# RWKV chunk tail and scan: a dense dummy matmul in every job and every step, and the scan's preparation spread anew

## The chip, the cores and the metric

The program runs on one core of one Trainium2 chip. The metric is device time in microseconds (us) of one execution; lower is better.

## The reference: what is computed

One layer of a diffusion backbone on 1152 tokens (1024 of a sample, 128 of a prompt): a SwiGLU half step, a mixer, another SwiGLU half step, with norms between. The mixer adds a Fourier group and a bidirectional RWKV-7 group with 8 heads of 64 channels. The change lies in the RWKV group, whose core is this scan, run forward and in reverse for every head:

```python
def step(state, inp):
    r_t, w_t, k_t, v_t, kk_t, a_t = inp
    sa = jnp.einsum('bhvk,bhk->bhv', state, -kk_t)
    state = (state * w_t[:, :, None, :]
             + sa[..., None] * (kk_t * a_t)[:, :, None, :]
             + v_t[..., None] * k_t[:, :, None, :])
    return state, jnp.einsum('bhvk,bhk->bhv', state, r_t)
```

kk is k scaled and divided by its norm in each head; w and a come from small products (64 wide) through a sigmoid.

## The kernel before

The heads are taken two at a time, as four pairs p = 0 to 3, one after the other. The 1152 tokens are 18 chunks of 64 (NCH = 18). Each pair goes through three stages, and a stage begins only when every engine has ended the one before:

- **rw_chunks** makes what each chunk needs by itself. TensorE (PE) works through a list of jobs written out by hand, each a handful of small matmuls into one of eight PSUM banks (12 f32 matmuls in an f, w or y job, 6 in a u job), and ScalarE (ACT) or VectorE (DVE) copies each bank out. Meanwhile DVE inverts small triangular matrices, first for direction 0, then for direction 1. The list ends with two tails, one for each direction: 3 f jobs, 3 w jobs, 6 u jobs and 3 y jobs. The f jobs of a direction need DVE's inverse (`nat0_1`, `nat1_1`), and four dummy matmuls of 512 columns stand before that wait (`keep_clock(pe, sb, out, 4)`).
- **rw_scan** runs the 18 chunks in order, both directions (d) in turn. In step i PE makes S (old state times the chunk's keys, L1753), DVE adds to it (L1797), PE makes M from it (L1762), and DVE makes the new state (L1804) with GpSimd's decayed old one (L1817). Y is two more groups on PE (L1767, L1771), and ACT copies it out (L1826). S of a step needs M of the step before from DVE, and ACT's copy of Y, for its PSUM bank. PE's order is S0, S1, M0, Y0, M1, Y1.
- **rw_turn** finishes the pair and turns the prepared data of the next one into scan operands.

For p = 0 to 2 the scan also prepares the next pair, in class **Prep**: at the end of each step PE, ACT and DVE do the pieces that a table gives them. PE has 16 pieces, one in each of steps 1 to 16: `ss` (sums of squares, 9 matmuls with 128x128 weights and 2 columns, L1149, after ACT's `sq`), six `a`, six `w` (one matmul of 384 columns, L1228), and three `kk` (3 matmuls of 128 columns, L1157). DVE has passes over 128x1152 (`kd`, `ak`, `kds`, `rkk`: L1285, L1288, L1297, L1300) and two scans (`scan0`, `scan1`, L1292). **rw_first** runs the same pieces alone for the first pair.

An f32 matmul is two instructions in the trace, each with a weight load (PEld).

Of the kernel before, what the change touches and what calls it, by code (L numbers as in the profile page):

```python
# [8 lines left out]
ALU = mybir.AluOpType  # L9
# [5 lines left out]
P = 128  # L15
# [5 lines left out]
NT = T // P  # L21
# [106 lines left out]
    return pe.matmul(out, w_hi, x_hi, start=False, stop=stop)  # L128


def keep_clock(pe, sb, out, n):

    for _ in range(n):
        pe.matmul(out, sb["cst"][:, C_ID:C_ID + P], sb["cst"][:, 0:512], start=True, stop=True)


def parts(c):
# [1005 lines left out]
    return t[:, ::-1] if d else t  # L1143


def head_sums(pe, sb, ps, x):

    for t in range(NT):
        last = pe.matmul(ps[:, 2 * t:2 * t + 2], x[:, t * P:(t + 1) * P], sb["cst"][:, C_BLK:C_BLK + P:HS],  # L1149
                         start=True, stop=True)  # L1150
    return last
# [15 lines left out]
PP = {n: i for i, n in enumerate(("w0_0", "w0_1", "a0_0", "a0_1", "k_k", "k_a", "r_k", "ln_w", "ln_b", "one_ka"))}  # L1167


class Prep:  # L1170

    ITEMS = ["ss"] + [f"{n}_{c}" for n in ("a0", "kk", "w0", "a1", "w1") for c in range(NC)]

    def __init__(self, st, io, sb, rw, zd, p, ps):

# [5 lines left out]

    def items(self, i):

        return self.ITEMS[i - 1:i] if i else []

    def act_names(self, i):
        out = [x for x in self.items(i) if x[0] in "wa"]
        return out + {2: ["sqrt"], 5: ["kda0"], 14: ["kda1"]}.get(i, [])  # L1190

    def dve_names(self, i):
        out = [x for x in self.items(i) if x[0] not in "wa"]
        return out + {3: ["inv", "wide"], 6: ["kd0"], 9: ["ak0"], 12: ["scan0"], 15: ["kd1"], 16: ["ak1"],
                      17: ["kds", "rkk", "scan1"]}.get(i, [])

    def of(self, name):
        return (self.act_t if name[0] in "wa" else self.dve_t)
# [12 lines left out]
    def pe(self, pe, i):  # L1211
        rw = self.rw
        for name in self.items(i):
            n = self.ITEMS.index(name)
            if n >= 2:
                before = self.ITEMS[n - 2]
                self.of(before).wait(pe, before)
            bank = self.ps[:, n % 2, :]
            if name == "ss":
                self.act_t.wait(pe, "sq")  # L1220
                last = head_sums(pe, self.sb, bank, rw.sq[:, :])
            else:
                c = int(name[-1])
                if name[0] in "wa":
                    d, which = int(name[1]), "wa".index(name[0])
                    rows = slice(HS * d, HS * d + HS)
                    pe.wait_ge(self.w_in[which], 16)
                    last = pe.matmul(bank[:, 0:CW], (rw.w2, rw.a2)[which][rows, :], rw.lora[rows, which, c * CW:(c + 1) * CW],  # L1228
                                     start=True, stop=True)
                else:  # L1230
                    self.dve_t.wait(pe, "wide")
                    last = spread(pe, self.sb, bank, rw.sq[:, :], c)
            self.pe_t.did(name, last)

    def act(self, act, i):
        rw, t = self.rw, self.act_t
        if i == 0:
            act.wait_ge(self.z_in[1], 16)
            self.dve_t.wait(act, "ka1")
            t.did("kraw", act.activation(rw.kk[:, :], rw.rkv[:, 1, :], ACT.Identity, scale=self.par("k_k")))  # L1240
            t.wait(act, "kraw")
            t.did("sq", act.activation(rw.sq[:, :], rw.kk[:, :], ACT.Square))
        for name in self.act_names(i):
            if name == "sqrt":
                self.dve_t.wait(act, "ss")
                t.did(name, act.activation(rw.inv[:, :], rw.inv[:, :], ACT.Sqrt))
            elif name.startswith("kda"):
                d = int(name[-1])
                t.wait(act, f"a{d}_{NC - 1}")
                t.did(name, act.activation(rw.bk[:, d, :, 1, :], by_chunk(rw.ai[d]), ACT.Identity, bias=self.par("one_ka"),  # L1250
                                           scale=self.par("k_a")))
            else:
                d, c = int(name[1]), int(name[-1])
                self.pe_t.wait(act, name)
                dst = (rw.sw if name[0] == "w" else rw.ai)[d]
                t.did(name, act.activation(dst[:, c * CW:(c + 1) * CW], self.ps[:, self.ITEMS.index(name) % 2, 0:CW],
                                           ACT.Sigmoid, bias=self.par(f"{name[0]}0_{d}")))

    def dve(self, dve, i):
# [7 lines left out]
            t.did("ka1", dve.tensor_scalar(self.par("one_ka"), self.par("k_a"), -1.0, 1.0, ALU.mult, ALU.add))  # L1267
        for name in self.dve_names(i):
            d = int(name[-1]) if name[-1].isdigit() else None
            if name == "ss":  # L1270
                self.pe_t.wait(dve, "ss")
                ins = dve.tensor_scalar(rw.inv[:, :], self.ps[:, 0, 0:2 * NT], 1e-24, None, ALU.max)
            elif name == "inv":
                self.act_t.wait(dve, "sqrt")
                ins = dve.reciprocal(rw.inv[:, :], rw.inv[:, :])
# [3 lines left out]
            elif name.startswith("kk_"):  # L1279
                self.pe_t.wait(dve, name)  # L1280
                cols = slice(d * CW, (d + 1) * CW)
                ins = dve.tensor_tensor(rw.kk[:, cols], self.ps[:, self.ITEMS.index(name) % 2, 0:CW], rw.kk[:, cols], ALU.mult)
            elif name.startswith("kd") and d is not None:
                self.act_t.wait(dve, f"kda{d}")
                ins = dve.tensor_tensor(rw.bk[:, d, :, 1, :], rw.bk[:, d, :, 1, :], by_chunk(rw.rkv[:, 1, :]), ALU.mult)  # L1285
            elif name.startswith("ak"):
                t.wait(dve, f"kk_{NC - 1}")
                ins = dve.tensor_tensor(rw.bk[:, d, :, 0, :], by_chunk(rw.ai[d]), by_chunk(rw.kk[:, :]), ALU.mult)  # L1288
            elif name.startswith("scan"):
                t.wait(dve, f"ak{d}")  # L1290
# [182 lines left out]
def rw_chunks(nc, io, sb, rw, nd, wd):  # L1473
# [44 lines left out]
    with Stage(nc) as st, nc.psum_tensor(fresh("g_ps"), [P, 8, 512], F32) as ps:  # L1518
# [10 lines left out]
        with st.block() as block:  # L1529
# [37 lines left out]
            def _(pe):  # L1567
                for n, (k, d, q) in enumerate(jobs):
# [31 lines left out]
                                             start=True, stop=True)  # L1600
                    elif k == "f":
                        if q == 0:
                            keep_clock(pe, sb, out, 4)
                            dve_t.wait(pe, f"nat{d}_1")
                        for j in range(NF):
                            u = q * NF + j
                            last = pe.matmul(out[second(d), j * B:(j + 1) * B], gu[first(d), d, u, second(d)],
                                             nat[d][first(d), u, :], start=True, stop=True)
                    elif k == "w":
                        copied(pe, "f", d, q)  # L1610
                        for j in range(NF):
                            u = q * NF + j
                            last = pe.matmul(out[first(d), j * B:(j + 1) * B], fs[d][second(d), u * B:(u + 1) * B],
                                             wu[second(d), d, u, second(d)], start=True, stop=True)
                    elif k == "u":
                        copied(pe, "z", d, q)
                        copied(pe, "w", d, q * NU // NF)
                        for j in range(NU):
                            u = q * NU + j
                            last = pe.matmul(out[0:HS, j * HS:(j + 1) * HS], wu[:, d, u, :], su[0:HS, d, u, :],  # L1620
                                             start=True, stop=True)
                    else:
                        copied(pe, "a", d, NG - 1)
                        for m in (1, 2):
                            copied(pe, "w", d, m)
                        for j in range(NU):
                            c = q * NU + j
                            for h in range(2):
                                last = pe.matmul(out[HS * h:HS * h + HS, j * HS:(j + 1) * HS],
                                                 at[:, d, c, HS * h:HS * h + HS], rw.wt[:, d, h, c, :], start=True, stop=True)  # L1630
                    pe_t.did(name(k, d, q), last)

            def copy_out(eng, tr, k, d, q, copy, neg):

# [90 lines left out]
def rw_scan(nc, io, sb, rw, zd, p, more):  # L1725
# [4 lines left out]
    SD = [(i, d) for i in range(NCH) for d in range(2)]  # L1730
    y = [rw.work[:, d * T:(d + 1) * T] for d in range(2)]
    with Stage(nc) as st, nc.psum_tensor(fresh("c_ps"), [P, 8, 512], F32) as ps:
        pe_t = Steps(st.sem("pe_s"), [x for i in range(NCH) for x in (f"S{i}_0", f"S{i}_1", f"M{i}_0", f"Y{i}_0", f"M{i}_1", f"Y{i}_1")] +
                     ["st0", "st1"])
        dve_t = Steps(st.sem("dve_s"), ["zero"] + [x for i in range(NCH) for x in
                                                   [f"S{i}_0", f"S{i}_1"] + [f"M{i}_0", f"M{i}_1"]])
# [5 lines left out]
        with st.block() as block:  # L1742
            @block.tensor
            def _(pe):
# [9 lines left out]
                                         old(i, d)[rows], start=True, stop=True)  # L1754
                    pe_t.did(f"S{i}_{d}", last)

                def rest(i, d):
                    c = order[d][i]
                    dve_t.wait(pe, f"S{i}_{d}")
                    for h in range(2):  # L1760
                        rows = slice(HS * h, HS * h + HS)
                        last = pe.matmul(ps[rows, 4 + d, 0:HS], rw.bt[:, d, c, HS * h:HS * h + HS],  # L1762
                                         rw.sv[:, d, h, c, :], start=True, stop=True)
                    pe_t.did(f"M{i}_{d}", last)
                    for h in range(2):
                        rows = slice(HS * h, HS * h + HS)
                        pe.matmul(ps[rows, 2 * d + h, HS:2 * HS], rw.sv[:, d, h, c, :], rw.gr[:, d, h, c, HS:2 * HS],  # L1767
# [3 lines left out]
                        last = pe.matmul(ps[rows, 2 * d + h, HS:2 * HS], old(i, d)[rows],  # L1771
                                         rw.ar[rows, d, 1, c * HS:(c + 1) * HS], start=False, stop=True)
                    pe_t.did(f"Y{i}_{d}", last)
                for i, d in SD:
                    s_part(i, d)
                    if d:
                        rest(i, 0)
                        rest(i, 1)
                        if more:
                            prep.pe(pe, i)  # L1780
                for d in range(2):

                    act_t.wait(pe, f"Y{NCH - 1}_{d}")
# [194 lines left out]
```

## Time and profile before

| | us |
|---|---|
| runs: median (lowest to highest) | 3276.66 (3276.38 to 3277.37) |
| the profiled execution | 3270.4 |
| its span, first to last instruction | 3268.6 |
| PE busy in the span | 2870.4 (88%) |
| DVE / ACT / GpSimd busy | 1469.9 / 782.3 / 105.2 |
| mean granted TensorE clock | 0.857 of full |

The four pairs lie between 1399.4 and about 2250 us of the span. PEclk in the page and in the answers is the clock that was granted to TensorE, as a share of full speed: 1.00 is 2.4 GHz and 0.50 is 1.2 GHz. The instruction rows give the start and the stretch of a merged group, then engine, line, operation, tiles, shapes and count; in brackets stands the idle time before it and what ended it.

### The profile page before, as it was taken

To read this page: it belongs to the slowest core of one execution; us is meant where nothing else is said; L and a number is where in the kernel's file an instruction comes from. 1 tells how busy PE (TensorE), PEld (TensorE's weight loads), DVE (VectorE), ACT (ScalarE), POOL (GpSimd) and SP (SyncE) were. 2 spreads that over 40 slices of the span, in tenths; PEclk is the share of its full clock that TensorE was granted. 3 is DMA by queue.
4 is the path that set the end of the run, shared out by engine and by line. 5 is a ranking of instruction groups with operands and counts; after the bars stand their busy time and mean duration, and the time that the engine had idled before them with its cause. 6 is when DMAs were issued, how large, how long until landed. Compare 5 with 4: busy or idle time off the path is not lost. (4 is left out here: it accounts for less than half of the span.)

```text
span 3268.6 us, 47367 instructions
## 1 busy us (share of the span) xinstructions
PE 2870.4 (88%) x18974; PEld 2642.3 (81%) x18974; DVE 1469.9 (45%) x2799; ACT 782.3 (24%) x1527; POOL 105.2 (3%) x165
## 2 busy tenths in 40 slices
PE   4599999999996999579689688786889999999995
PEld 2289999999995998266476575666789999999995
DVE  1453333333437661382563745733364433333335
ACT  1231111111104111333243433322141111111112
POOL 0000000000000000001102001010000000000000
PEclk7799999999997999765665655657889999999997
DMA  8511111111101232111010110104111111111101
GB/s 350 208 52 39 39 39 39 51 39 50 40 7 40 82 96 106 76 24 31 18 23 24 25 39 3 34 5 162 39 49 42 45 39 39 39 39 51 39 19 58
DMA packets 190799, 182.69 MB, mean 56 GB/s; under 512 B 43956, under 2 KB 163551, under 8 KB 190687
## 3 DMA queue, kind: packets, MB, share of 16 engines
q1 hardware_dynamic: 190416, 180.97, 17.1%
q8 instruction: 87, 1.43, 0.2%
q14 instruction: 26, 0.21, 0.0%
q10 hardware_dynamic: 270, 0.09, 0.0%
HBM read 153.05 MB, written 27.98 MB: 55 GB/s over the span
## 5 line engine op out<-in xcount | busy, mean ns | idle before, releaser
L126 PE MATMUL ff_ps<-h_hi,ff_wlo 128*128 128x384 f32 x2112 | 710.7, 336 | 5.6 <-ACT ff_s L602 5.6
L127 PE MATMUL ff_ps<-h_lo,ff_whi 128*128 128x384 f32 x2112 | 709.9, 336 | 0.0
L128 PE MATMUL ff_ps<-h_hi,ff_whi 128*128 128x384 f32 x2112 | 709.6, 336 | 0.0
L650 DVE TENSOR_TENSOR ff_s<-ff_ps,ff_s 128x384 f32<-128x384 f32 x132 | 73.5, 557 | 750.0 <-PE ff_ps L128 748.7
L126 PEld LDWEIGHTS ff_ps<-h_hi,ff_wlo 128*128 128x128 f32 x2112 | 400.2, 189 | 6.2 <-ACT ff_s L602 6.2
L127 PEld LDWEIGHTS ff_ps<-h_lo,ff_whi 128*128 128x128 f32 x2112 | 399.8, 189 | 0.0
L128 PEld LDWEIGHTS ff_ps<-h_hi,ff_whi 128*128 128x128 f32 x2112 | 399.7, 189 | 0.0
L128 PE MATMUL ff_ps<-ff_uhi,ff_whi 128*128 128x384 f32 x1056 | 352.7, 334 | 0.0
L127 PE MATMUL ff_ps<-ff_ulo,ff_whi 128*128 128x384 f32 x1056 | 352.7, 334 | 0.0
L126 PE MATMUL ff_ps<-ff_uhi,ff_wlo 128*128 128x384 f32 x1056 | 352.7, 334 | 0.0
L602 ACT ACTIVATE ff_s<-ff_ps 128x384 f32<-128x384 f32 x132 | 65.1, 493 | 738.4 <-PE ff_ps L128 738.4
L661 DVE SCALAR_TENSOR_TENSOR x_again<-ff_ps,mod,x_again 128x256 f32<-128x256 f32 (+1 forms) x352 | 171.1, 514 | 72.1 <-PE ff_ps L128 71.4
L661 DVE SCALAR_TENSOR_TENSOR x<-ff_ps,mod,x 128x256 f32<-128x256 f32 (+1 forms) x352 | 171.0, 514 | 72.1 <-PE ff_ps L128 71.4
L606 ACT ACTIVATE ff_uhi<-ff_s 128x384 fp32r<-128x384 f32 x132 | 69.4, 526 | 556.1 <-DVE ff_s L650 556.1
L127 PEld LDWEIGHTS ff_ps<-ff_ulo,ff_whi 128*128 128x128 f32 x1056 | 198.2, 188 | 0.0
L128 PEld LDWEIGHTS ff_ps<-ff_uhi,ff_whi 128*128 128x128 f32 x1056 | 198.2, 188 | 0.0
L126 PEld LDWEIGHTS ff_ps<-ff_uhi,ff_wlo 128*128 128x128 f32 x1056 | 198.2, 188 | 0.0
L643 DVE TENSOR_TENSOR ff_wlo<-ff_raw,ff_whi 128x1024 fp32r<-128x1024 f32 x132 | 157.5, 1219 | 17.7 <-ACT ff_whi L597 17.5
L126 PE MATMUL pj_ps<-h_hi,pj_wlo 128*128 128x384 f32 x456 | 154.2, 338 | 1.5 <-DVE h_lo L464 1.5
L127 PE MATMUL pj_ps<-h_lo,pj_whi 128*128 128x384 f32 x456 | 153.2, 336 | 0.0
L128 PE MATMUL pj_ps<-h_hi,pj_whi 128*128 128x384 f32 x456 | 153.1, 336 | 0.0
L597 ACT ACTIVATE ff_whi<-ff_raw 128x1024 fp32r<-128x1024 f32 x132 | 131.8, 1044 | 0.0
(269 smaller groups left out, 3759.4 us busy)
## 6 DMA issues: line engine op xcount, KB each, us to landing
md_w<-w_mod SPq DMA_DIRECT2D x9, 4096.0 KB, 24.6
ff_raw<-ffn_w_gate SPq DMA_DIRECT2D x44, 512.0 KB, 4.6
ff_raw<-ffn_w_up SPq DMA_DIRECT2D x44, 512.0 KB, 3.9
ff_raw<-ffn_w_down SPq DMA_DIRECT2D x44, 512.0 KB, 3.7
pj_raw<-w_in SPq DMA_DIRECT2D x19, 512.0 KB, 4.0
z_dram<-pj_zo SPq DMA_DIRECT2D x15, 576.0 KB, 2.9
rw_rkv<-z_dram SPq DMA_DIRECT2D x12, 576.0 KB, 5.6
x_dram<-x SPq DMA_DIRECT2D x1, 4608.0 KB, 21.7
```

The costliest lines, as they stand in the source:

```text
L126: pe.matmul(out, w_lo, x_hi, start=start, stop=False)
L127: pe.matmul(out, w_hi, x_lo, start=False, stop=False)
L128: return pe.matmul(out, w_hi, x_hi, start=False, stop=stop)
L597: act.activation(w_hi[:, u, :], raw[:, u % RAW, :], ACT.Copy).then_inc(w_hi_s, 1)
L602: act.activation(silu[:, t % 2, :], ps[:, t % 2, 0:CW], ACT.Silu).then_inc(gate_free, 1)
L606: act.activation(hid_hi[:, m, c * CW:(c + 1) * CW], hid[:, t % 2, :], ACT.Copy).then_inc(hid_hi_s, 1)
L643: dve.tensor_tensor(w_lo[:, u, :], raw[:, u % RAW, :], w_hi[:, u, :].bitcast(F32), ALU.subtract)\
L650: dve.tensor_tensor(hid[:, t % 2, :], ps[:, 2 + t % 2, 0:CW], silu[:, t % 2, :], ALU.mult)\
L661: last = dve.scalar_tensor_tensor(xs, ps[:, 4 + n % 4, a:b], sb["mod"][:, (3 * (2 * f) + 2) * KD + o, s:s + 1], xs, ALU.mult, ALU.add)
```

## The change

1. `keep_clock` takes a number of columns. A dummy multiplies the 128x128 identity with `columns` columns of the constants, into a bank that is written anew afterwards.
2. In rw_chunks every f, w, u and y job of both directions (15 in each) begins with a dummy of 128 columns. The f jobs keep the four of 512 as well. After the last job PE waits for the copy of the eighth-last job and makes two dummies of 512 columns.
3. In rw_scan every step of all four pairs gets a dummy of 256 columns behind S0 and S1, and PE's order becomes S0, S1, dummy, M0, M1, Y0, Y1.
4. Prep's pieces are laid out in three tables. `ss` is cut into three pieces of 3 matmuls, in steps 1 to 3, each together with an `a0` piece; `kk` goes to steps 7 to 9, `w` to 10 to 15. On DVE `kd1`, `kds`, `rkk`, `scan0` and `scan1` move to steps 8, 13, 14, 15 and 16 (they were in 15, 17, 17, 12 and 17). On ACT `sqrt` moves from step 2 to 4, `kda1` from 14 to 7.

```diff
-def keep_clock(pe, sb, out, n):
+def keep_clock(pe, sb, out, columns, n=1):
     for _ in range(n):
-        pe.matmul(out, sb["cst"][:, C_ID:C_ID + P], sb["cst"][:, 0:512], start=True, stop=True)
+        pe.matmul(out[:, 0:columns], sb["cst"][:, C_ID:C_ID + P], sb["cst"][:, 0:columns], start=True, stop=True)
...
+PREP_PE = {1: ("ss_0", "a0_0"), 2: ("ss_1", "a0_1"), 3: ("ss_2", "a0_2"), 4: ("a1_0", ), 5: ("a1_1", ), 6: ("a1_2", ),
+           7: ("kk_0", ), 8: ("kk_1", ), 9: ("kk_2", ), 10: ("w0_0", ), 11: ("w0_1", ), 12: ("w0_2", ),
+           13: ("w1_0", ), 14: ("w1_1", ), 15: ("w1_2", )}
+PREP_ACT = {4: ("sqrt", ), 5: ("kda0", ), 7: ("kda1", )}
+PREP_DVE = {1: ("ss_0", ), 2: ("ss_1", ), 3: ("ss_2", ), 5: ("inv", "wide"), 6: ("kd0", ), 8: ("kk_0", "kd1"), 9: ("kk_1", ),
+            10: ("kk_2", ), 11: ("ak0", ), 12: ("ak1", ), 13: ("kds", ), 14: ("rkk", ), 15: ("scan0", ), 16: ("scan1", )}
...
-    ITEMS = ["ss"] + [f"{n}_{c}" for n in ("a0", "kk", "w0", "a1", "w1") for c in range(NC)]
+    ITEMS = [name for i in sorted(PREP_PE) for name in PREP_PE[i]]
...
                         if q == 0:
-                            keep_clock(pe, sb, out, 4)
+                            keep_clock(pe, sb, out, 512, 4)
                             dve_t.wait(pe, f"nat{d}_1")
+                        keep_clock(pe, sb, out, P)
...
                     elif k == "w":
+                        keep_clock(pe, sb, out, P)
                         copied(pe, "f", d, q)
...
                     elif k == "u":
+                        keep_clock(pe, sb, out, P)
                         copied(pe, "z", d, q)
...
                     else:
+                        keep_clock(pe, sb, out, P)
                         copied(pe, "a", d, NG - 1)
...
                     pe_t.did(name(k, d, q), last)
+                copied(pe, *jobs[-8])
+                keep_clock(pe, sb, ps[:, len(jobs) % 8, :], 512, 2)
...
-                for i, d in SD:
-                    s_part(i, d)
-                    if d:
-                        rest(i, 0)
-                        rest(i, 1)
-                        if more:
-                            prep.pe(pe, i)
+                for i in range(NCH):
+                    for d in range(2):
+                        s_part(i, d)
+                    keep_clock(pe, sb, ps[:, 4, P:3 * P], 2 * P)
+                    for part in (m_part, y_part):
+                        for d in range(2):
+                            part(i, d)
+                    if more:
+                        prep.pe(pe, i)
```

## Rows read from the trace of the kernel before

**Rows 1.** The page, part 2: the span in 40 slices.

```profile
PEclk7799999999997999765665655657889999999997
```

**Rows 2.** Busy time by stage; columns PE, PEld, DVE, ACT, POOL, PEclk, DMA share, GB/s.

```profile
1399.40:1496.90 97.50, 82.72 (x978) 72.78 (x978) 64.10 (x160) 32.69 (x86) 5.89 (x4) 0.69 0.12 26
1496.90:1585.80 88.90, 78.08 (x644) 52.34 (x644) 34.66 (x89) 32.46 (x96) 21.74 (x36) 0.50 0.07 23
...
2148.80:2209.90 61.10, 50.37 (x584) 38.77 (x584) 20.42 (x73) 16.53 (x76) 15.89 (x36) 0.50 0.01 3
```

**Rows 3.** Timeline of PE in pair 0, both tails of the chunk stage.

```profile
1454.22 3.88 PE L1607 MATMUL g_ps<-rw_rkv,rw_gr 32*32 32x32 f32 x69 [5.44 <-DVE rw_rkv L1706]
...
1461.85 7.83 PE L1620 MATMUL g_ps<-rw_sv,rw_wt 64*64 64x64 f32 x71
...
1469.53 4.09 PE L1629 MATMUL g_ps<-rw_wt,rw_bk 64*64 64x64 f32 x71
1473.56 6.17 PE L134 MATMUL g_ps<-cst 128*128 128x512 f32 x8
1479.66 2.37 PE L1607 MATMUL g_ps<-rw_sq,rw_gr 32*32 32x32 f32 x69
...
1484.23 6.89 PE L1620 MATMUL g_ps<-rw_sv,rw_wt 64*64 64x64 f32 x71
...
1490.97 4.09 PE L1629 MATMUL g_ps<-rw_wt,rw_bk 64*64 64x64 f32 x71
```

**Rows 4.** Busy time and granted clock in short stretches, columns as in rows 2.

```profile
1441.00:1444.40 3.40, 3.40 (x62) 3.40 (x60) 2.88 (x13) 3.00 (x8) 0.00 (x0) 1.00 0.00 0
1454.20:1473.50 19.30, 19.28 (x288) 19.15 (x288) 14.20 (x40) 6.76 (x14) 0.00 (x0) 0.50 0.06 18
1473.50:1478.60 5.10, 5.10 (x8) 2.19 (x7) 2.01 (x2) 0.49 (x1) 0.00 (x0) 0.50 0.36 58
1478.60:1482.00 3.40, 3.40 (x80) 2.53 (x79) 1.27 (x2) 0.48 (x1) 0.00 (x0) 1.00 0.00 0
1482.00:1485.40 3.40, 3.40 (x96) 3.36 (x92) 0.55 (x1) 1.67 (x4) 0.00 (x0) 1.00 0.02 5
```

**Rows 5.** Timeline of PE in pair 0's scan, a step with a `kk` piece.

```profile
1523.04 0.48 PE L1762 MATMUL c_ps<-rw_sv,rw_bt 128*64 128x64 f32 x4
1523.30 0.43 PE L1767 MATMUL c_ps<-rw_gr,rw_sv 128*64 128x64 f32 x4
1523.66 0.48 PE L1771 MATMUL c_ps<-rw_ar,rw_m 64*64 64x64 f32 x4
1524.07 1.65 PE L1157 MATMUL c_ps<-cst,rw_sq 128*128 128x128 f32 x6
1525.64 0.69 PE L1753 MATMUL c_ps<-rw_m,rw_ar 64*64 64x64 f32 x8
1526.56 0.48 PE L1762 MATMUL c_ps<-rw_sv,rw_bt 128*64 128x64 f32 x4 [0.22 <-DVE rw_sv L1797]
```

**Rows 6.** Timeline in pair 3's scan, which has no preparation.

```profile
2152.60 0.48 PE L1753 MATMUL c_ps<-rw_m,rw_ar 64*64 64x64 f32 x4 [0.43 <-DVE rw_sv L1797]
...
2154.67 0.37 PE L1771 MATMUL c_ps<-rw_ar,rw_m 64*64 64x64 f32 x2
...
2155.20 0.45 ACT L1826 ACTIVATE rw_work<-c_ps 64x64 f32<-64x64 f32 x2 [0.59 <-PE c_ps L1771]
...
2155.79 0.48 PE L1753 MATMUL c_ps<-rw_m,rw_ar 64*64 64x64 f32 x4 [0.43 <-DVE rw_sv L1797]
```

**Rows 7.** Timeline of pair 0's scan: its start, and the wait for `sq`.

```profile
1497.12 0.70 PE L1753 MATMUL c_ps<-rw_m,rw_ar 64*64 64x64 f32 x8 [2.06 <-DVE rw_m L1792]
...
1503.68 4.00 PE L1149 MATMUL c_ps<-cst,rw_sq 128*128 128x2 f32 x18 [0.37 <-ACT rw_sq L1242]
```

**Rows 8.** Timeline at the end of pair 0's scan.

```profile
1581.31 0.38 SPq L1846 DMA_DIRECT2D state_b<-rw_mp  x1
1582.00 2.55 DVE L1292 TENSOR_TENSOR_SCAN rw_wt<-rw_reset,rw_wt 128x1152 f32<-128x1152 bf16 x1
```

More of the change, by code:

```diff
@@ L1143, in reverse, with head_sums @@
     return t[:, ::-1] if d else t
-def head_sums(pe, sb, ps, x):
-    for t in range(NT):
+def head_sums(pe, sb, ps, x, tiles=range(NT)):
+    for t in tiles:
         last = pe.matmul(ps[:, 2 * t:2 * t + 2], x[:, t * P:(t + 1) * P], sb["cst"][:, C_BLK:C_BLK + P:HS],
@@ L1184, in items @@
     def items(self, i):
-        return self.ITEMS[i - 1:i] if i else []
+        return list(PREP_PE.get(i, ()))
     def act_names(self, i):
         out = [x for x in self.items(i) if x[0] in "wa"]
-        return out + {2: ["sqrt"], 5: ["kda0"], 14: ["kda1"]}.get(i, [])
+        return out + list(PREP_ACT.get(i, ()))
     def dve_names(self, i):
-        out = [x for x in self.items(i) if x[0] not in "wa"]
-        return out + {3: ["inv", "wide"], 6: ["kd0"], 9: ["ak0"], 12: ["scan0"], 15: ["kd1"], 16: ["ak1"],
-                      17: ["kds", "rkk", "scan1"]}.get(i, [])
+        return list(PREP_DVE.get(i, ()))
     def of(self, name):
@@ L1218, in pe @@
             bank = self.ps[:, n % 2, :]
-            if name == "ss":
+            if name.startswith("ss"):
                 self.act_t.wait(pe, "sq")
-                last = head_sums(pe, self.sb, bank, rw.sq[:, :])
+                j = int(name[-1])
+                last = head_sums(pe, self.sb, bank, rw.sq[:, :], range(j * NC, (j + 1) * NC))
             else:
@@ L1244, in act @@
             if name == "sqrt":
-                self.dve_t.wait(act, "ss")
+                self.dve_t.wait(act, "ss_2")
                 t.did(name, act.activation(rw.inv[:, :], rw.inv[:, :], ACT.Sqrt))
@@ L1269, in dve @@
             d = int(name[-1]) if name[-1].isdigit() else None
-            if name == "ss":
-                self.pe_t.wait(dve, "ss")
-                ins = dve.tensor_scalar(rw.inv[:, :], self.ps[:, 0, 0:2 * NT], 1e-24, None, ALU.max)
+            if name.startswith("ss"):
+                self.pe_t.wait(dve, name)
+                cols = slice(d * 2 * NC, (d + 1) * 2 * NC)
+                ins = dve.tensor_scalar(rw.inv[:, cols], self.ps[:, self.ITEMS.index(name) % 2, cols], 1e-24, None, ALU.max)
             elif name == "inv":
@@ L1287, in dve @@
                 t.wait(dve, f"kk_{NC - 1}")
+                self.act_t.wait(dve, f"a{d}_{NC - 1}")
                 ins = dve.tensor_tensor(rw.bk[:, d, :, 0, :], by_chunk(rw.ai[d]), by_chunk(rw.kk[:, :]), ALU.mult)
@@ L1732, in rw_scan @@
     with Stage(nc) as st, nc.psum_tensor(fresh("c_ps"), [P, 8, 512], F32) as ps:
-        pe_t = Steps(st.sem("pe_s"), [x for i in range(NCH) for x in (f"S{i}_0", f"S{i}_1", f"M{i}_0", f"Y{i}_0", f"M{i}_1", f"Y{i}_1")] +
+        pe_t = Steps(st.sem("pe_s"), [x for i in range(NCH) for x in (f"S{i}_0", f"S{i}_1", f"M{i}_0", f"M{i}_1", f"Y{i}_0", f"Y{i}_1")] +
                      ["st0", "st1"])
@@ L1755, in s_part, with m_part @@
                     pe_t.did(f"S{i}_{d}", last)
-                def rest(i, d):
+                def m_part(i, d):
                     c = order[d][i]
@@ L1764, in rest, with y_part @@
                     pe_t.did(f"M{i}_{d}", last)
+                def y_part(i, d):
+                    c = order[d][i]
                     for h in range(2):
```

## Prediction, written before the changed kernel ran

> **What bounds the kernel now.** I read the page's slices first. The clock granted to TensorE is near full at both ends and drops to a half for long parts of slices 18 to 27, where the four pairs lie [rows 1]. A table by stage says where: in the chunk stage the mean grant is 0.69, in both kinds of scan it is 0.50, though PE is busy for 78 of 89 us and 50 of 61 us [rows 2]. So these stages are set by small matmuls at 1.2 GHz and by the hand-overs between engines. The change buys a faster clock with extra PE work. Two questions decide: what a dummy costs, and whether the clock comes.
>
> **The price of a dummy.** It stands in no row, so I build it. In the first tail 72 instructions of 64 columns take 1461.85 to 1469.53, 0.107 us each at the slow clock [rows 3]; 128 columns are then 0.21 us, and a dummy of 128 columns (two instructions) streams for 0.43 us. But a group with 128x128 weights among small ones costs more than its stream. The six instructions of a `kk` piece stream for 1.28 us, and the next group starts 1.57 us after their first: 0.29 us more. Ahead of it, the four instructions of L1771 hold PE for 0.41 us, where the four of L1762 take 0.26 us: another 0.15 us [rows 5]. I take 0.43 + 0.44, about 0.88 us at the slow clock and 0.44 at the fast. The bound below is the stream alone, 0.43 and 0.21 us, if the loads hide; the bound above is 0.95, since a 32x32 group may be slower to restart.
>
> These rows speak against a load that hides. The Trainium skill (TensorE: Matmul & The Clock Gate, Part 2, step 1) says that a weight load is pulled ahead of running matmuls only when its row groups don't conflict or it goes to a background buffer. If it went there, a dummy would cost its stream, and the kernel would land at the second rival below.
>
> **First tail of the chunk stage (direction 0).** PE has no gap in it: 19.3 us busy of 19.3, clock 0.50 [rows 4]. Nothing hides the dummies: 15 x 0.88 = 13.2 us. The wide dummies and the f jobs of direction 1 stand behind it, and DVE's inverse was ready when they came (6.1 us later) [rows 3]. I take 13.0 us, since a wide dummy may see the fast clock a little sooner.
>
> **Second tail.** It begins at the fast clock, which the four wide dummies brought (5.1 us dense at 0.50, then 1.00) [rows 4]. But in before the clock held only to 1485.4, though PE never paused: f1 and w1 are 32x32 [rows 3, 4]. With a dummy in each job, a job is 4.57 / 6 = 0.76 us of small work and 0.44 us of dummy, of which only 0.21 streams. That is a sixth of the time dense, the rest at 32x32, and I take it as too thin: nearest to it is the stretch that lost the clock. A stretch of only 64x64 work (the z jobs) kept it [rows 4], so u and y jobs would hold it, if it lived so long. So: four f and w jobs fast, 4 x 1.2 = 4.8 us; two slow, at 7.63 / 6 + 0.88 = 2.15 each, 4.3; six u at 1.28 + 0.88, 13.0; three y at 1.35 + 0.88, 6.7. Sum 28.8 us, against 15.4 (1479.66 to 1495.06): +13.4. The two dummies of 512 columns at the end are 4 x 0.85 + 0.3 = 3.7 us, less the copy of the last job that they run beside, under 1 us: +2.8.
>
> A pair's chunk stage: 13.0 + 13.4 + 2.8 = +29.2 us; four pairs: **+117**.
>
> **Scan of pairs 0 to 2.** A step of 4.55 us is M, Y, Y twice (0.26 + 0.36 + 0.41, twice), the piece 1.57, and S to M 0.92 [rows 5]. PE is nearly the whole of it. New, slow clock: S 0.38, then 0.24 to the dummy, then 256 columns twice at 0.43 with 0.29 around them, 1.77 in all from S to M instead of 0.92. DVE's add no longer shows, which is the little that the dummy covers. M0 and M1 together save 0.05. So +0.8 a step, 18 steps: +14.4. The cut `ss` adds two changes of weights, +0.5. The later passes of DVE fit beside steps of 5.3 us, so a stall of about a pass (1.3 us) goes, and the stage no longer ends on `kds`, `rkk`, `scan1` (to 1584.55) but on the store of the states issued at 1581.31 [rows 8]: -1.2. Sum +12.4, three pairs **+37**.
>
> Could it run fast? The stage starts with a hole: PE's `ss_0` waits for ACT's `sq` until 1503.68, 6.6 us after the start [rows 7], and at the fast clock two steps are done by 5 us. The hole, and then matmuls of two columns, lose the clock if it was there. In the slow clock the `kk` steps come nearest to winning it back: 1.28 us dense, S, then 0.85 us dense. 1.28 alone never did in before; 5.1 did [rows 4, 5]. I give each scan even odds. A fast step is half of 5.35, about 2.7 us, since PE is nearly all of it. From step 8 on, eight such steps are worth 20 us. The likeliest count is one or two of three: **-28**.
>
> **Scan of pair 3.** A step is 3.19 us (2152.60 to 2155.79), and what ends the wait is ACT's copy of Y1: from the start of Y1's last group to the next S1 it is 1.12 us [rows 6]. The dummy comes behind S1, so it lies on this chain. New period: 1.12, then S1 to dummy 0.40, dummy 1.14, M 0.48, Y0 and Y1 up to that last group 0.36 + 0.77: 4.27 us. 18 x 1.08 = **+19.5**. I take the slow clock: the end of the chunk stage leaves a gap of over 1.5 us before the scan's first S.
>
> rw_first runs the same pieces in the new order, with the same work: within 2 us of none.
>
> **Sum.** 117 + 37 - 28 + 19.5 = +146 us. On the profiled execution's 3270.4 that is 3416; the median of the runs is 6.3 above it, so 3423. I say **3423 us**. Less than 0.2% (7 us) is what a measurement here can't tell from no change.
>
> **Rivals.**
> *The clock holds (faster).* It decides in one place: whether f and w jobs with their dummies keep 1.00 in the second tail, and then the dummies before and in the scan carry it on. Then the second tail is 6 x 1.2 + 6 x 1.08 + 3 x 1.12 = 17.1 us, +1.7; the end +1.0; with 13.0 a pair pays 15.7, four 63. The scans of pairs 0 to 2 run 16 steps at 2.7 instead of 4.55 us, -30, and lose 2 to DVE's longer passes, -28 each; pair 3's chain at 2.7 us (its 3.15 us of PE work halve, of the 1.12 about 1.0 stays, since most of it is ACT), -9. Sum 63 - 84 - 9 = -30: 3247 us. For it: the z jobs' stretch. Against: 1482.0 to 1485.4, PE busy throughout, and the fall behind it [rows 4]. The Trainium skill (the same page, the part on why this matters) asks only that TensorE be kept busy without long gaps; by that rule the second tail would have stayed fast in before too, and the trace differs. Chance 0.12.
>
> *The loads hide.* A dummy costs its stream: first tail +6.4; second 22.2 us, +6.8; end +2.5, four pairs 63. Scans +5 each, pair 3 +12. Sum +90: 3367 us. Against: rows 5 name both extras. Chance 0.07.
>
> *The tail is slow, the scans fast.* The wide dummies at the stage's end bring the clock and it is held: 117 - 93 = +24, 3301 us. The hole at `sq` [rows 7] stands against it for three pairs. Chance 0.07.
>
> *Nothing moves,* gains and costs cancel: 0.02.
>
> **How the numbers follow.** My case has 0.72. Its own range: no scan won back is 3451, all three 3391; a dummy at 0.95 adds 15; 3380 to 3470. The range for 8 in 10 goes down to take in the loads that hide and part of what lies between: 3325 to 3470. Faster 0.12, same 0.02, slower 0.86.
>
> **What would show it.** In the profile after: 0.9 us between the small groups around each dummy in the first tail, and f1 some 13 us later after f0; the grant falling before w1 ends; PEclk 0.50 at step 2 of pairs 0 to 2; steps of 5.3 us, and of 4.3 in pair 3. I'm wrong if the second tail shows 1.00 to its end, if scan steps of 2.7 us fill a stage, or if a dummy costs 0.5 us.

## The result, and the profile after

| | before | after |
|---|---|---|
| median of the runs (us) | 3276.52 (3275.04 to 3277.37) | 3372.74 (3370.30 to 3378.87) |
| ratio, 95% interval | | 1.0297 (1.0279 to 1.0315) |
| the profiled execution / its span | 3270.4 / 3268.6 | 3378.9 / 3377.1 |

The changed kernel is 96 us slower (a prediction of 3423, range 3325 to 3470, against 3372.74). The profiled execution of after is 108.5 us longer than that of before; it lies 6.1 us above its median where before's lay 6.1 below.

The page's slices of after. Between slices 18 and 27 the grant (the clock granted to TensorE) is only a little higher than in [rows 1], digits that average 6.2 against 5.5; the four pairs last longer.

```profile
PEclk7699999999998998567756756767979999999997
...
L134 PE MATMUL g_ps<-cst 128*128 128x128 f32 (+1 forms) x320 | 140.0, 553 | 21.2 <-DVE rw_rkv L1721 21.2
```

The table by stage of after, chunk stage and scan in turn for pairs 0 to 3 (columns as in [rows 2]). A chunk stage runs here from GpSimd's clearing of its tiles to DVE's clearing of `rw_m`, the scan from there to DVE's first addition in rw_turn.

```profile
1402.05:1528.07 126.02, 112.04 (x1042) 92.60 (x1042) 64.12 (x161) 32.72 (x86) 5.89 (x4) 0.64 0.09 20
1528.07:1612.32 84.25, 76.94 (x680) 49.25 (x680) 33.26 (x91) 32.61 (x97) 26.70 (x36) 0.71 0.07 25
1640.98:1771.76 130.78, 113.17 (x1042) 92.09 (x1042) 64.09 (x160) 32.72 (x86) 5.89 (x4) 0.63 0.09 19
1771.76:1857.84 86.08, 80.39 (x680) 51.81 (x680) 33.35 (x92) 32.62 (x97) 26.66 (x36) 0.68 0.07 24
1886.48:2017.46 130.98, 113.24 (x1042) 92.14 (x1042) 64.09 (x160) 32.72 (x86) 5.89 (x4) 0.63 0.09 19
2017.46:2103.53 86.07, 80.40 (x680) 51.79 (x680) 33.35 (x91) 32.63 (x97) 26.66 (x36) 0.68 0.07 24
2131.99:2258.45 126.46, 112.40 (x1042) 92.74 (x1042) 64.17 (x161) 32.72 (x86) 5.89 (x4) 0.64 0.10 20
2258.45:2313.99 55.54, 46.86 (x620) 31.95 (x620) 18.81 (x73) 16.55 (x76) 15.38 (x36) 1.00 0.01 3
```

By the same marks the stages of before last 97.5, 100.6, 101.0, 98.4 us (chunk) and 89.0, 88.7, 88.5, 61.4 us (scan). So:

| stages of four pairs, us | before | after | measured | predicted |
|---|---|---|---|---|
| rw_chunks | 397.5 | 514.3 | +116.8 | +117 |
| scans of pairs 0 to 2 | 266.2 | 256.4 | -9.8 | +37 - 28 = +9 |
| scan of pair 3 | 61.4 | 55.5 | -5.8 | +19.5 |

That is +101.2 us. The other 7.3 of the 108.5 lie outside these stages: 2.6 before the first chunk stage, 0.1 in the three rw_turn between pairs, 4.6 behind the last scan. The change touches none of that code but rw_first, which has the new order of pieces. The profiled executions with the new order reach the first chunk stage between 1398.9 and 1402.1 us, and that of e2 below, with the old one, at 1401.5, so the order doesn't explain the 2.6 us. I take the 7.3 us for a property of these two executions; the medians are 96 us apart.

PE's timeline in pair 0's tails (f1 and w1 are the f and w jobs of direction 1): a slow f job of the first tail, then the start of the second tail, then the end of the list.

```profile
1459.10 0.80 PE L134 MATMUL g_ps<-cst 128*128 128x128 f32 x2
1459.83 1.49 PE L1617 MATMUL g_ps<-rw_rkv,rw_gr 32*32 32x32 f32 x24
1461.24 0.80 PE L134 MATMUL g_ps<-cst 128*128 128x128 f32 x2
...
1489.56 5.03 PE L134 MATMUL g_ps<-cst 128*128 128x512 f32 x10
1494.53 0.94 PE L1617 MATMUL g_ps<-rw_sq,rw_gr 32*32 32x32 f32 x24
1495.40 0.49 PE L134 MATMUL g_ps<-cst 128*128 128x128 f32 x2
...
1498.39 1.31 PE L1624 MATMUL g_ps<-rw_wt,rw_rkv 32*32 32x32 f32 x24
1499.64 0.80 PE L134 MATMUL g_ps<-cst 128*128 128x128 f32 x2
...
1523.68 3.10 PE L134 MATMUL g_ps<-cst 128*128 128x512 f32 x4
1528.29 0.45 PE L1768 MATMUL c_ps<-rw_m,rw_ar 64*64 64x64 f32 x8 [1.51 <-DVE rw_m L1812]
```

A slow job takes 1461.24 - 1459.10 = 2.14 us, where [rows 3] gave 7.63 / 6 = 1.27: the dummy costs 0.87 us. The first tail is 32.6 us (1456.96 to 1489.56) against 19.3. The wide dummies take 5.0 us instead of 6.1, the second tail 29.2 us (1494.53 to 1523.68) against 15.4, and from there to the scan's start it is 4.4 us against 1.8: +13.3, -1.1, +13.8 and +2.6, in all +28.5 us. By the marks above the four chunk stages grow by 28.5, 30.2, 30.0 and 28.0 us.

Busy time and granted clock in pair 0: the second tail's start and its rest, the scan's start, its middle, its end.

```profile
1491.80:1498.60 6.80, 6.80 (x92) 4.73 (x91) 0.55 (x1) 0.96 (x2) 0.00 (x0) 1.00 0.01 2
1498.70:1526.00 27.30, 27.30 (x237) 22.43 (x235) 2.75 (x5) 3.39 (x7) 0.00 (x0) 0.50 0.00 1
1526.00:1536.20 10.20, 6.50 (x77) 4.16 (x75) 2.40 (x11) 4.05 (x10) 2.62 (x6) 1.00 0.54 190
1536.20:1580.60 44.40, 44.40 (x293) 28.03 (x294) 11.96 (x38) 16.34 (x41) 7.69 (x14) 0.50 0.00 1
1580.60:1607.90 27.30, 26.08 (x316) 16.71 (x312) 18.91 (x42) 10.99 (x41) 16.40 (x16) 1.00 0.00 1
```

The grant falls in w1's first job, is back for the end dummies and the scan's first steps, falls at the wait for `sq`, and comes back at 1580.60, behind the second `kk` piece and the dummy of the step after it. These are the rows where it falls and rises (ACT, PE), and the dummies of two steps after it:

```profile
1534.20 1.16 ACT L1249 ACTIVATE rw_sq<-rw_kk 128x1152 f32<-128x1152 f32 x1
...
1535.42 0.83 PE L1149 MATMUL c_ps<-cst,rw_sq 128*128 128x2 f32 x6 [1.88 <-ACT rw_sq L1249]
...
1573.60 1.22 PE L134 MATMUL c_ps<-cst 128*128 128x256 f32 x2
...
1576.82 1.65 PE L1157 MATMUL c_ps<-cst,rw_sq 128*128 128x128 f32 x6
...
1579.02 1.22 PE L134 MATMUL c_ps<-cst 128*128 128x256 f32 x2
...
1581.63 0.94 PE L1157 MATMUL c_ps<-cst,rw_sq 128*128 128x128 f32 x6
...
1586.01 0.70 PE L134 MATMUL c_ps<-cst 128*128 128x256 f32 x2
...
1589.14 0.70 PE L134 MATMUL c_ps<-cst 128*128 128x256 f32 x2
```

A slow step with one piece is 1579.02 - 1573.60 = 5.42 us, a fast one 1589.14 - 1586.01 = 3.13 us. Scans 1 and 2 begin slow, since the end dummies of these pairs didn't raise the grant, and win the clock at the same place. Pair 3 holds 1.00 through its whole scan, with steps of 2.89 us (S1 to S1, against 3.19 in [rows 6]):

```profile
2261.67 0.33 PE L1768 MATMUL c_ps<-rw_m,rw_ar 64*64 64x64 f32 x4 [0.20 <-ACT rw_work L1846]
2261.93 0.70 PE L134 MATMUL c_ps<-cst 128*128 128x256 f32 x2
...
2264.56 0.33 PE L1768 MATMUL c_ps<-rw_m,rw_ar 64*64 64x64 f32 x4 [0.20 <-ACT rw_work L1846]
```

### The profile page after: what moved, and what is told of

It is laid out like the page before. It is cut to its first block and busy times, and to the rows that moved or that the text cites. A ratio compares the mean times of both kernels' runs of the same rounds, so it can differ in the third digit from the quotient of the medians.

```text
span 3377.1 us, 48143 instructions
## 1 busy us (share of the span) xinstructions
PE 3000.9 (89%) x19374; PEld 2714.8 (80%) x19374; DVE 1464.3 (43%) x2807; ACT 782.7 (23%) x1527; POOL 119.5 (4%) x165
## 5 line engine op out<-in xcount | busy, mean ns | idle before, releaser
L134 PE MATMUL g_ps<-cst 128*128 128x128 f32 (+1 forms) x320 | 140.0, 553 | 21.2 <-DVE rw_rkv L1721 21.2
```

The costliest lines, as they stand in the source:

```text
L134: pe.matmul(out[:, 0:columns], sb["cst"][:, C_ID:C_ID + P], sb["cst"][:, 0:columns], start=True, stop=True)
```

## The experiments

The stage lengths of every profiled execution, by the same marks. It is one execution of each kernel, and it lies 25 us above the kernel's median in e1, 9 above in e5, 14 below in e7, 11 below in e12 and 10 below in e13; in the others within 7 us. F stands for a scan at 1.00 but for its last microseconds, K for one that won the clock back in the `kk` steps, S for one that was at 0.50 but for a start of under 15 us (e13's pair 2 had a stretch of 7 us at 1.00 besides).

| run | median us | ratio (interval) | four chunk stages | scans, pairs 0 to 3 |
|---|---|---|---|---|
| before | 3276.5 | | 397.5 | 89.0 S, 88.7 S, 88.5 S, 61.4 S |
| after | 3372.7 | 1.0297 (1.0279 to 1.0315) | 514.3 | 84.2 K, 86.1 K, 86.1 K, 55.5 F |
| e1_no_tail | 3274.7 | 0.9990 (0.9968 to 1.0012) | 410.5 | 99.9 S, 99.5 S, 82.5 K, 55.5 F |
| e2_tail_only | 3383.1 | 1.0321 (1.0304 to 1.0338) | 501.8 | 90.2 S, 90.1 S, 89.9 S, 61.3 S |
| e3_second_tail_only | 3350.3 | 1.0239 (1.0201 to 1.0277) | 464.8 | 84.8 K, 86.1 K, 86.1 K, 81.9 S |
| e4_order_prep | 3272.9 | 0.9980 (0.9967 to 0.9993) | 401.8 | 87.0 S, 86.6 S, 86.7 S, 65.3 S |
| e5_wide_in_fw | 3328.3 | 1.0128 (1.0075 to 1.0181) | 434.1 | 84.4 K, 84.8 K, 101.3 S, 81.9 S |
| e7_two_columns | 3367.5 | 1.0294 (1.0255 to 1.0334) | 496.5 | 83.4 K, 83.5 K, 84.2 K, 55.6 F |
| e8_hole_filled | 3259.5 | 0.9955 (0.9938 to 0.9971) | 410.3 | 66.3 F, 84.8 K, 66.3 F, 80.8 S |
| e9_hole_and_ss | 3261.5 | 0.9946 (0.9919 to 0.9973) | 413.4 | 88.3 K, 67.9 F, 88.2 K, 55.5 F |
| e11_start_dense | 3223.1 | 0.9833 (0.9820 to 0.9847) | 412.7 | 67.1 F, 67.1 F, 67.1 F, 57.2 F |
| e10_best | 3218.6 | 0.9821 (0.9807 to 0.9834) | 407.8 | 67.8 F, 67.1 F, 67.1 F, 57.1 F |
| e12_no_scan_dummies | 3389.1 | 1.0352 (1.0334 to 1.0369) | 513.5 | 87.1 S, 76.0 K, 87.6 S, 64.9 S |
| e13_best_no_scan_dummies | 3274.5 | 0.9992 (0.9978 to 1.0007) | 407.1 | 84.0 S, 78.8 K, 80.9 S, 65.4 S |

**Which dummies cost.** e1 takes the 30 of the tails out of after, e2 puts them alone into before, e3 keeps those of direction 1.

```diff
-                        keep_clock(pe, sb, out, P)
```

This is e1, in the f, w, u and y jobs; e3 has in its place:

```diff
-                        keep_clock(pe, sb, out, P)
+                        if d == 1:
+                            keep_clock(pe, sb, out, P)
```

> The changed kernel without the 30 dummies of 128 columns in the tails' jobs; the dummies at the end of the list, those of the scan and the new preparation stay. Theory A (a tail dummy only costs: 0.87 us at the slow clock each, and what the scans gained comes from the end dummies and the scan's own): the four chunk stages give back 13.0 + about 13.5 us each, so about 3373 - 106 = 3267 us, with pair 3's scan at 1.00 and about 55.5 us and the scans of pairs 0 to 2 at 84 to 86 us. Theory B (the tail dummies are what lets the scans win their clock, by handing over a denser stretch): the chunk stages give back the same 106, but the scans go back to 88.7 and 61.4 us, about 3283 us. Theory C (PE's dummies lay beside a wait in the tails): less than half of the 106 comes back, over 3320 us.

> The kernel before plus the 30 tail dummies of 128 columns alone: no end dummies, old scan order, old preparation. Theory A: +106 us, about 3383 us, the scans as in before (88.7 us at 0.50, pair 3 61.4 us). Theory B: the scans gain about 16 us in all, about 3367 us. Theory C (the 106 us of the chunk stages come from the end dummies or the handover to the scan): under 3330 us.

> The changed kernel with tail dummies in direction 1 alone. Theory A (each tail pays for its own dummies): 15 x 0.87 = 13.0 us come back in each pair's first tail and the second tail keeps its 28 to 29 us, about 3373 - 52 = 3321 us. Rival (the second tail starts earlier and is then caught by the wait for the inverse of direction 1 or by the copies): less than 8 us a pair comes back, over 3341 us.

Windows of e2, its first chunk stage and scan:

```profile
1401.46:1525.42 123.96, 109.98 (x1038) 92.06 (x1038) 64.28 (x160) 32.83 (x86) 5.89 (x4) 0.64 0.10 20
1525.42:1615.65 90.23, 78.06 (x644) 52.30 (x644) 34.67 (x90) 32.49 (x97) 21.75 (x36) 0.50 0.07 23
```

The tail dummies alone cost 501.8 - 397.5 = 104.3 us and give no scan anything, its scans are even 4 us longer in sum: Theory A (106 us; that the median is 3383 to the microsecond is luck). Without them (e1) the chunk stages give back 103.8 us; of the new dummies only the two at the end are left there, +13.0 us for four pairs. e3 gives 49.5 us back in its chunk stages, where 52 were due. But e1 came 8 us over and e3 29 us over their expectations. In the profiled executions that stands in the scans: 337.5 us in e1, whose profiled execution is the slowest of ten, and 338.8 in e3, against 311.9 in after. Windows of e1: pair 1's scan up to where the grant falls, its rest, and pair 3's scan; under them that of e3's pair 3.

```profile
1734.47:1744.00 9.53, 7.51 (x86) 5.03 (x86) 3.04 (x14) 6.02 (x12) 2.62 (x6) 0.99 0.58 201
1744.00:1833.99 89.99, 85.77 (x596) 53.47 (x594) 30.68 (x77) 26.58 (x85) 23.63 (x30) 0.50 0.01 2
2179.20:2234.72 55.52, 46.87 (x620) 31.95 (x620) 18.80 (x73) 16.54 (x76) 15.38 (x36) 1.00 0.01 3
```

```profile
2206.34:2288.21 81.87, 72.63 (x620) 49.38 (x620) 19.22 (x73) 16.53 (x76) 15.38 (x36) 0.50 0.01 2
```

The same scan code takes 55.5 us at 1.00 and 81.9 at 0.50 in pair 3; 82 to 86 us when the clock comes in the `kk` steps and 99 to 101 when it doesn't. In pair 3 of e3 the end dummies never raised the grant. One kernel gives both: pairs 0 and 1 of e1 stay slow and pair 2 wins the clock, and e1's ten runs lie between 3261 and 3300 us, before's beside them between 3269 and 3281.

**Order and preparation alone.** e4 is after without all its new dummies.

> The changed kernel without any of its new dummies (tails, end, scan): the new order of PE and the new spread of the preparation alone. Theory A (the clock in the scans comes from the new dummies): all four scans run at 0.50; the spread takes away a stall and shortens the end, -2 to -4 us for each of pairs 0 to 2, pair 3 within 1 us, about 3276.5 - 9 = 3267 us. Rival (moving the kk pieces into three steps in a row is what wins the clock back): the scans of pairs 0 to 2 show 1.00 in their last steps and are shorter by 10 us or more each, about 3240 us.

Its pair 3, all of it at the slow clock:

```profile
2146.67:2211.99 65.32, 55.91 (x584) 41.73 (x584) 20.41 (x74) 16.53 (x76) 15.86 (x36) 0.50 0.01 3
```

No scan shows 1.00, so moving the `kk` pieces didn't win the clock here; with the same scan code one of e12's three did (below). The scans of pairs 0 to 2 are 5.9 us shorter together, where 9 were due, and the new order costs 3.9 us in pair 3 (steps of 3.42 us instead of 3.19), which I had put at nothing. That accounts for a median of 3273 and not 3267. The chunk stages, whose code is that of before, came out 4.3 us longer in this execution: differences of that size between two rows of the table show nothing. The new order and the new spread were not run apart in pairs 0 to 2.

**What a dummy costs.** e7 cuts the tail dummies to 2 columns (`keep_clock(pe, sb, out, 2)`).

> The changed kernel with the 30 tail dummies cut to 2 columns: what is left is their weight load and the change of tile size. In after a slow f, w, u or y job with a dummy of 128 columns took 0.87 us more than without. Theory A (0.43 of it is the stream, the rest is fixed): 0.44 us a dummy, first tail 19.3 + 6.6 = 25.9 us, the chunk stage 12 to 13 us over the same kernel without tail dummies, about 3320 us. Rival 1 (the load hides, and the price is a multiple of the stream): 0.05 us or less, first tail under 20.5 us. Rival 2 (the price is a floor whatever the columns): 0.87 us, first tail 32.4 us, about 3373 us.

A slow w job of e7, PE's timeline:

```profile
1462.66 0.59 PE L134 MATMUL g_ps<-cst 128*128 128x2 f32 x2
1463.18 1.49 PE L1624 MATMUL g_ps<-rw_wt,rw_rkv 32*32 32x32 f32 x24
1464.59 0.59 PE L134 MATMUL g_ps<-cst 128*128 128x2 f32 x2
```

The job is 1.93 us, 0.66 more than without a dummy, with next to nothing to stream. e7's first tail is 29.5 us, where Theory A has 25.9 and Rival 2 has 32.4. So the price lies between them: 0.66 us are there with 2 columns, and the 0.43 us that 128 columns stream add only 0.21. Whether the 0.66 is the weight load or the change of tile size, e7 doesn't separate. From 128 to 256 columns (e5 below, at the slow clock: 1.15 us from the dummy's start to the next group's against 0.73) the whole 0.42 is added. At the fast clock a job takes 1.19, 1.29 and 1.50 us with 2, 128 and 256 columns, and 0.76 without.

The Trainium skill (TensorE: Matmul & The Clock Gate, LDWEIGHTS) puts a weight load at its columns over 1.2 in ns, about 0.11 us for 128; by that page I estimate 0.21 us for the two loads of an f32 dummy. The trace shows that this is not the price: the 2-column dummy holds PE for 0.52 us before the next group starts, and the job pays 0.66.

**Can small work hold the clock in the second tail?** e5 gives the f and w jobs of direction 1 dummies of 256 columns, and the other tail jobs none.

```diff
+                        if d == 1:
+                            keep_clock(pe, sb, out, 2 * P)
```

> The changed kernel with dummies of 256 columns in the six f and w jobs of direction 1, none in the other tail jobs; end and scan dummies kept. The prediction took a sixth of the time at 128x128 as too thin to hold the clock; here it is 0.43 of 1.4 us. Theory A (how much of the time streams through the full array decides): the second tail stays at 1.00, 6 x 1.41 + 6 x 0.64 + 3 x 0.68 = 14.4 us against 15.4, the chunk stage about 2 us over before (of which 3 are the end dummies). Rival (32x32 work between loses it whatever stands beside it): the grant falls in w1 as before, four of six jobs pay up to 1.3 us, the chunk stage is 6 to 9 us over before.

Windows of e5: the second tail of pair 0, most of that of pair 1, and pair 2's scan behind its first 2.3 us.

```profile
1480.80:1500.00 19.20, 17.93 (x306) 13.89 (x304) 3.42 (x7) 4.36 (x9) 0.00 (x0) 1.00 0.01 2
1702.80:1723.00 20.20, 20.20 (x201) 16.41 (x200) 2.76 (x5) 3.40 (x7) 0.00 (x0) 0.50 0.01 2
...
1951.80:2050.85 99.05, 94.63 (x652) 59.34 (x650) 32.42 (x85) 32.51 (x97) 25.41 (x34) 0.50 0.05 17
```

In pair 0 the grant stays to the end, with a second tail of 14.8 us where 14.4 were expected; in pairs 1 and 2 it falls in w1 and in pair 3 already in the second f job. Neither theory holds: with 256 columns one second tail of four held it. With 128 columns none of 16 did (after, e2, e3, e12), with 384 columns all eight did (e10, e13).

**Where the scans lose it.** e8 is e1 with three dummies of 256 columns ahead of the wait for `sq`; e9 has two more ahead of each of `ss_1` and `ss_2`. `self.fill` is true in the scan and false in rw_first.

```diff
             if name.startswith("ss"):
+                if self.fill:
+                    keep_clock(pe, self.sb, bank[:, P:3 * P], 2 * P, 3 if name == "ss_0" else 0)
                 self.act_t.wait(pe, "sq")
```

> The changed kernel without tail dummies, and with three dummies of 256 columns ahead of the wait for sq in the scans of pairs 0 to 2. In the run without tail dummies these scans began at 1.00 and fell to 0.50 9.4 us in, behind an idle stretch of 1.36 us at that wait and one of 0.52 us for a weight load. Theory A (the hole is what loses the clock): the three scans keep 1.00, 18 steps of about 3.1 us, 58 us instead of 82 to 100, the program at about 3195 us. Rival (the two thin pieces behind it, 6 instructions of 2 columns and 2 with 64 rows in each of steps 1 to 3, lose it by themselves): the grant falls a step or two later, the scans stay at 82 to 99 us, 3270 us.

> As the kernel before it, and with two dummies of 256 columns ahead of ss_1 and ss_2 too (steps 2 and 3). At the fast clock they cost 2 x 2 x 0.45 = 1.8 us a scan. Theory A (hole alone): 2 us a pair slower than the kernel before it, about 3200 us. Rival (the thin pieces lose the clock): this one keeps 1.00 where that one doesn't, about 3200 us against 3270.

The four scans of e8:

```profile
1501.68:1568.03 66.35, 60.09 (x686) 39.58 (x686) 32.95 (x91) 32.41 (x97) 26.19 (x36) 0.96 0.09 31
1700.41:1785.26 84.85, 79.22 (x686) 51.25 (x686) 33.11 (x91) 32.59 (x97) 27.90 (x36) 0.71 0.07 24
1918.44:1984.79 66.35, 59.95 (x686) 39.76 (x686) 32.96 (x92) 32.39 (x97) 26.19 (x36) 0.96 0.09 31
2113.77:2194.54 80.77, 71.50 (x620) 48.68 (x620) 19.19 (x73) 16.53 (x76) 15.37 (x36) 0.51 0.01 2
```

Both kernels missed Theory A's 3195 and 3200 us by 60 and more, and lie nearer the rival's 3270; the windows say why it is still the hole. It was one place: without a filler all six scans that came to it at 1.00 lost the clock there (three of e1, one each of after, e5 and e7), and with it all three of e8 and e9 kept it (66.3 us in e8), thin pieces behind it or not. The extra fillers of e9 only add 1.5 us. The miss has two parts: such a scan takes 66.3 us and not 58, and there is a second place: in e8's pairs 1 and 3 and e9's pairs 0 and 2 the grant fell 1.7 to 2.3 us after the scan's start, behind the idle 1.5 us between the stages. e11 therefore adds `keep_clock(pe, sb, ps[:, 4, P:3 * P], 2 * P, 4)` ahead of the first S, and e10 has the f and w dummies of e5 too, with 384 columns.

> The kernel with the hole at sq filled and no tail dummies, plus four dummies of 256 columns at the very start of the scan of every pair. With the hole filled, two of four scans kept 1.00 to near their end (66.3 us), and two lost it 1.7 and 2.1 us after the start, just behind the idle 1.5 us between the stages. Theory A (that gap is the second place where the clock is lost): all four scans run at 1.00, 67.2 us for pairs 0 to 2 and 56.4 for pair 3, the chunk stages at about 103 us as there: 3276.5 + 13 - 65 - 5 = about 3220 us, with runs closer together. Rival (the level at the start is chance, and dense work behind the gap does not change it): one or two of four scans still drop, 3255 us as there.

> The kernel just described, plus dummies of 384 columns in the f and w jobs of direction 1. With 256 columns one of four second tails kept 1.00 to its end. Theory A (more of the time at 128x128 holds it): all four second tails stay at 1.00: 6 x 1.71 + 6 x 0.73 + 3 x 0.75 = 16.9 us against 15.4, the end dummies 2.0 instead of 3.8 us, so the chunk stages as in the other kernel within 1 us a pair, and about 3218 us in all. Rival (32x32 work loses it in three pairs of four): f and w jobs at the slow clock pay up to 1.7 us each, the chunk stages are 6 us or more above the other kernel's in most pairs, 3240 us or more.

Scans of pairs 0 and 3 of e11, and a second tail with its end of e10:

```profile
1501.28:1568.41 67.13, 61.26 (x694) 40.70 (x694) 32.95 (x91) 32.46 (x97) 26.19 (x36) 0.98 0.09 31
...
2099.63:2156.80 57.17, 48.70 (x628) 33.31 (x628) 18.83 (x74) 16.59 (x76) 15.37 (x36) 0.99 0.01 3
```

```profile
1479.90:1500.60 20.70, 19.49 (x307) 14.13 (x306) 3.60 (x7) 4.35 (x9) 0.00 (x0) 1.00 0.01 2
```

All eight scans of the two runs are fast. e10 is the fastest kernel here, 3218.6 us, 58 us under before and 154 under after; its step over e11 (4.6 us in the medians) isn't clear, since their intervals overlap.

**Are the scan's own dummies needed?** e12 is after without them, e13 is e10 without them.

> The changed kernel without the dummy of 256 columns in the scan steps; tail and end dummies, the new order and preparation stay. Theory A (the scan dummies win the clock back in the kk steps and hold it in pair 3): no scan of pairs 0 to 2 shows 1.00 after its start, each is at 87 us as in the run with order and preparation alone; pair 3 starts at 1.00 and loses it, 60 to 65 us; chunk stages +117: about 3390 us. Rival (the end dummies bring it and the steps hold it by themselves): pair 3 runs at 1.00 through, under 52 us, and the program is at or under 3373 us.

> The kernel with all four fillers (3218.6 us) without the dummy of 256 columns in the scan steps. Theory A (the steps need it to hold the clock): the grant falls within a few steps, the scans of pairs 0 to 2 go to 80 us or more and pair 3 to 60 or more, about 3270 us. Rival (once the clock is there, steps with a piece hold it and the dummy only costs, 0.5 us a step at the fast clock): 72 x 0.5 = 36 us less, about 3183 us.

The windows of e13: pair 3's scan until the grant falls, and its rest.

```profile
2135.21:2141.60 6.39, 5.70 (x72) 4.25 (x72) 2.25 (x9) 1.15 (x6) 2.45 (x6) 1.00 0.00 0
2141.60:2200.63 59.03, 50.42 (x524) 37.42 (x522) 18.11 (x64) 15.44 (x71) 13.51 (x31) 0.50 0.01 3
```

Yes: both kernels are slower without them, by 16 us (e12) and 56 us (e13). In e12 all four scans begin at 1.00 and lose it within 2 us. One detail went against Theory A: e12's pair 1 and e13's pairs 1 and 2 won the clock again at or behind their `kk` steps without a dummy in the step. Over all profiled executions, of the scans of pairs 0 to 2 that were slow when they came to the `kk` steps, 15 of 18 won the clock with the step dummy and 3 of 15 without.

## Why the prediction was right, and where it was off

It was right that the tails pay and the scans don't pay it back. That the time lies in the stated range is in part luck: 3373 is below the range that I gave my own case (3380 to 3470) and inside only because that was stretched for the loads that hide, whose 3367 us it nearly hits by another road. One of my signs of being right failed (steps of 4.3 us in pair 3), and one of being wrong nearly came: steps of 2.89 us, where I had named 2.7, fill pair 3's scan.

- **The price of a dummy**, 0.88 us slow: 0.87 measured. The sum was right and its parts were not: 0.43 + 0.44 is really 0.66 + 0.21 (e7). The fast price, 0.44, was under: a fast job takes 1.29 us instead of 0.76, so 0.53. That changed little, as only the f jobs of direction 1 and part of a w job run fast.
- **First tail** +13.0: +13.3. **Second tail** +13.4: +13.8, with the grant falling in w1 as said. **End dummies** +2.8: +2.6 (e1: 3.3 a pair, with whatever else moved). The chunk term, +117, was +116.8; the closeness is in part luck, since the pairs differ (28.0 to 30.2 us) and in pairs 1 and 2 the end dummies didn't bring the clock. Rivals "the clock holds" and "the loads hide" fall here.
- **Scans of pairs 0 to 2, the slow step** of 5.35 us: 5.42. A scan that stays slow was to be 88.9 + 12.4 = 101.3 us; e5's pair 2 is just that, 101.3, and e1's, at 1.00 for the first 9.5 us, are 99.5 and 99.9.
- **The even odds in the `kk` steps** were the first step that failed: three of three scans won the clock, and 15 of 18 over all runs, not half. The size was off as well: a win leaves 86.1 us of 101.3, so 15 us, where I had 20, because a fast step is 3.13 us and not half of 5.35 (PE's groups don't halve: from S to the dummy 0.63 us becomes 0.38, the dummy's 1.15 becomes 0.63), and because the grant comes in step 9, behind the second `kk` piece. The sum had a slip too: even odds on three scans at 20 us are 30 us, not 28. In after the three scans come to -9.8 us, not +9.
- **Pair 3 at the slow clock**, +19.5, was the second and the larger: 25.3 us of the miss. Its price came out right (e3 and e5: 81.9 - 61.4 = +20.5; a step is 4.34 us, 4.27 forecast) through two errors that cancel: e4 puts 3.9 us on the new order, which I had at nothing, and so 16.6 are left for the dummy, 0.92 us a step where I had 1.14. The level was wrong. I reasoned that the gap of 1.5 us before the first S would lose the clock; in after it didn't, in e8 it did. In the runs with step dummies and nothing in the gap (after, e1, e3, e5, e7, e8, e9) 20 scans came to it at 1.00; 13 kept the clock over it and 7 lost it. I should have given this odds too.
- **The hole at `sq`** does what the prediction said: pair 0 loses the clock there, and with the hole filled a scan that reaches it at 1.00 keeps it (nine of nine in e8, e9, e11, e10).

The account against the predicted +146: chunk stages 0, scans of pairs 0 to 2 -19, pair 3 -25, the code outside these stages +7, together -37 us (measured +108.5 in the profiled executions). The medians are 50 us under the prediction, since after's profiled execution lies above its median and before's below.

So nearly all of the change's loss is the 30 tail dummies. They bought nothing that these runs show: e2 has them and no scan gains, and e1 without them has a scan of each fast kind (82.5 us in pair 2, 55.5 in pair 3). The scan dummies hold the clock (e12, e13), and they pay when the gap and the hole are filled (e11 against e1: 52 us). The end dummies bring 1.00 to the scan's door in 27 of the 35 stages that came to them slow, and not in after's pairs 1 and 2. No run takes them out alone, so what they are worth, above all behind e11's start fillers or e10's fast tail, isn't shown.

What stays open: why the same code keeps the clock over the gap in one pair and not in the next, and why e12's pair 1 won it. In e8, PE's rows of pair 0 (kept) and pair 1 (lost) show the same instructions, durations and idle 1.5 us from the end dummies to the third group after the first M, where one falls to 0.50. What does differ is when the grant rose. Of the 20 crossings above, it rose in one 19 us before the scan's start (kept). In the others it rose 0.56 to 0.96 us (seven scans) or 1.94 to 2.11 us (five) before it where it was kept, and 1.16 to 1.67 us (seven) where it was lost. With e11's fillers it was kept after 1.39 and 1.47 us too. So the level goes with where the rise falls against the gap, but no run sets that moment, and the cause isn't shown.

## What to carry to other kernels

Most of the price of a narrow dense dummy between small matmuls doesn't depend on its width (at the slow clock 0.66 us with 2 columns, 0.87 with 128, then 0.42 for the next 128), so few wide ones beat many narrow ones: 128 columns in every job cost 26 us a pair and brought nothing, 384 in six fast jobs held the clock at no cost that the runs can tell. Fill the whole chain or nothing: bring the clock up in front of a stage, cover each idle place in it, and check that the steps themselves hold it, or the dummies are paid at the slow clock. Where the level of a stage is decided by chance, run both levels' sums and give each pair its own odds.

## What the hardware showed that I had not expected

- The granted clock fell with PE never idle: in after's second tail PE is busy for 6.80 us of 6.80 at 1.00 and then for 27.30 of 27.30 at 0.50; in the scan it stays at 0.50 with PE busy for 44.40 us of 44.40. The Trainium skill (TensorE: Matmul & The Clock Gate, the part on why this matters) asks to keep TensorE busy; here busy with 32x32 and 64x64 work and a 128-column dummy in each job, or with scan steps and their 256-column dummy, was not enough.
- A 2-column f32 dummy with 128x128 weights costs a slow job of 32x32 matmuls 0.66 us; 128 columns cost 0.87.
- The steps with a 256-column dummy hold 1.00 in pair 3 for a whole scan, 55.5 us with PE busy for 46.9 (84%), while a tail busy all the time loses it.
